# Feature-major norms in a long one-core kernel: sums of squares with tokens on partitions, root and reciprocal on four columns, factors spread by a product with a diagonal

## What is computed

```python
def rmsnorm(x, g):
    xf = x.astype(jnp.float32)
    y = xf * lax.rsqrt(jnp.mean(xf * xf, axis=-1, keepdims=True) + EPS)
    return (y * g.astype(jnp.float32)).astype(x.dtype)
```

## Time and profile before

| | |
|---|---|
| median of three runs | 2881.63 us (2880.54 to 2885.57) |
| the profiled execution's own time | 2886.34 us |
| its span | 2884.3 us |
| mean granted TensorE clock | 0.895 |
| TensorE busy / VectorE busy / ScalarE busy | 2425.5 / 1237.0 / 937.1 us |
| chain that ended last: TensorE / DMA / VectorE / ScalarE | 59% / 29% / 7% / 3% |

### The profile page before, as it was taken

One profiled execution on the slowest core, in us unless ns is written; L12 is line 12 of the kernel. 1 busy time (PEld: TensorE's weight loads), 2 busy tenths in 40 slices (PEclk: granted clock), 3 DMA queues, 4 the chain that ended last, 5 costly groups with the idle time before them and its releaser, 6 DMA issues.

```text
span 2884.3 us, 37990 instructions
## 1 busy us (share of the span) xinstructions
PE 2425.5 (84%) x16498; PEld 1682.2 (58%) x16498; DVE 1237.0 (43%) x1751; ACT 937.1 (32%) x1522; POOL 60.1 (2%) x36
## 2 busy tenths in 40 slices
PE   7999998666666676666688889999999998987998
PEld 7897785111111111111367778889788787976787
DVE  4567652000010000000365655567754656855654
ACT  4556541000000000000244444445444443733442
POOL 0000010000000000000000000000000000022000
PEclk9999998867767777676898999999999999999999
DMA  6553467999999999999624246565655654422452
GB/s 214 172 149 132 132 234 310 418 418 416 416 418 418 418 417 416 418 418 418 249 91 116 89 137 213 193 214 164 215 194 180 200 175 161 143 68 76 161 194 98
DMA packets 309927, 698.09 MB, mean 242 GB/s; under 512 B 35425, under 2 KB 211809, under 8 KB 275073
## 3 DMA queue, kind: packets, MB, share of 16 engines
q1 hardware_dynamic: 307456, 681.78, 63.7%
q0 software_dynamic: 2016, 13.67, 1.3%
q10 hardware_dynamic: 288, 0.22, 0.0%
HBM read 694.58 MB, written 1.05 MB: 241 GB/s over the span
## 4 chain that ended last, share of the span: by engine, by line
PE 59%; DMA 29%; DVE 7%; ACT 3%; issue 1%; SPq 1%; DVEq 0%; ACTq 0%
PE ps L560 16%; PE ps L561 15%; PE ps L562 15%; DMA af<-in_w_exp_gate 12%; DMA af<-in_w_exp_up 10%; DMA af<-in_w_exp_down 6%; PE ps L1567 2%; PE ps L2328 1%; PE ps L1598 1%; DVE ar L533 1%; PE ps L828 1%; PE ps L1110 1%; PE ps L1949 1%; SPq L491 1%; PE ps L960 1%
## 5 line engine op out<-in xcount | busy, mean ns | idle before, releaser
L560 PE MATMUL ps<-ar 128*128 128x512 f32 (+1 forms) x2688 | 944.5, 351 | 45.5 <-ACT ar L850 17.5
L561 PE MATMUL ps<-ar 128*128 128x512 f32 (+1 forms) x2688 | 925.0, 344 | 0.0
L562 PE MATMUL ps<-ar 128*128 128x512 f32 (+1 forms) x2688 | 924.6, 344 | 0.0
L533 DVE TENSOR_TENSOR ar<-af,ar 128x1024 fp32r<-128x1024 f32 x520 | 610.6, 1224 | 317.3 <-ACT ar L522 317.0
L560 PEld LDWEIGHTS ps<-ar 128*128 128x128 f32 x2688 | 516.5, 192 | 123.9 <-DVE ar L873 13.8
L522 ACT ACTIVATE ar<-af 128x1024 fp32r<-128x1024 f32 x520 | 516.2, 1049 | 157.5 <-PE ps L562 154.6
L562 PEld LDWEIGHTS ps<-ar 128*128 128x128 f32 x2688 | 516.8, 192 | 59.1
L561 PEld LDWEIGHTS ps<-ar 128*128 128x128 f32 x2688 | 517.8, 193 | 55.7 <-issue 0.5
L1567 PE MATMUL ps<-af 128*32 128x512 f32 x2048 | 369.0, 818 | 183.9 <-DMA af<-in_w_exp_up 92.1
L1567 PEld LDWEIGHTS ps<-af 128*32 128x32 f32 x2048 | 50.9, 125 | 485.4 <-DMA af<-in_w_exp_up 237.0
L1598 PE MATMUL ps<-af 128*32 128x512 f32 x1024 | 176.1, 804 | 95.2 <-DMA af<-in_w_exp_down 81.1
(11 more groups left out here) (279 smaller groups left out, 1597.4 us busy)
## 6 DMA issues: line engine op xcount, KB each, us to landing
af<-in_w_exp_gate SPq DMA_DIRECT2D x128, 1024.0 KB, 25.4
af<-in_w_exp_up SPq DMA_DIRECT2D x128, 1024.0 KB, 24.8
af<-in_w_exp_down SPq DMA_DIRECT2D x128, 1024.0 KB, 21.4
af<-in_ffn_w_in SPq DMA_DIRECT2D x88, 1024.0 KB, 5.8
af<-in_ffn_w_out SPq DMA_DIRECT2D x44, 1024.0 KB, 5.1
af<-in_w_in SPq DMA_DIRECT2D x33, 1024.0 KB, 5.2
af<-in_sgu_w_in SPq DMA_DIRECT2D x16, 1024.0 KB, 7.1
af<-in_w_out SPq DMA_DIRECT2D x12, 1024.0 KB, 5.1
```

What stands on the lines that cost most here:

```text
L533: e.tensor_tensor(self.WL[load.pair][:, c], self.base(i)[:, c], f_(self.WH[load.pair][:, c]), ALU.subtract).then_inc(*self.dve.inc(("lo", ...
L560: e.matmul(o, lh, rh, start=start, stop=False, skip_group_check=True)
L561: e.matmul(o, lh, rl, start=False, stop=False, skip_group_check=True)
L562: return e.matmul(o, ll, rh, start=False, stop=stop, skip_group_check=True)
```

## The change

In t_rms the operands change places. The squares of 128 tokens are now the stationary operand and two columns of the matrix of 1/1024 are the moving one, so that 16 products of 2 columns (8 groups by 2 halves of the tokens) take the place of 8 products of 256 columns; the mean squares of the tokens land on partitions, in four columns of PSUM. The root (a_sd) and the reciprocal (v_rstd) are then taken of 128 x 4 values, in a small tile SD. To bring the factors back along the free axis on all partitions, VectorE builds two 128 by 128 diagonal matrices (identity times factor times 1024) in RSTD, and TensorE multiplies each by the matrix of 1/1024 (the new t_spread: two products of 128 columns) into a PSUM bank, which v_normed reads in place of RSTD. For mem the spread stands behind the first half of the projection dak; for the other six it stands right behind the sums. The bank for it is one more out of the ring, so dak's quarters are in other banks than before.

```diff
--- before.py
+++ after.py
@@ -252,7 +252,7 @@
-        self.RSTD, self.SM2 = sm[:, 512:768], sm[:, 768:1024]
+        self.RSTD, self.SM2, self.SD = sm[:, 512:768], sm[:, 768:1024], sm[:, 504:508]
         self.IDN = self.C("ident")
         self.where = {}
         self.plan()
@@ -820,15 +820,27 @@
 
 
     def t_rms(self, e, name, tmp, ring, fs=range(8), first=True, last=True):
+
         if first:
             self.rms_free = self.take(ring.next(), name, (self.act, (name, "sd")))
         for n, f in enumerate(fs):
-            for w in self.Tw.new(*self.rms_free, self.act.val((name, "sq", f // 2))):
-                e.wait_ge(*w)
-            m = e.matmul(self.bank(name)[:, 0:T], self.C("ones"), F(tmp)[:, f, :], start=first and n == 0, stop=last and n == len(fs) - 1,
-                         skip_group_check=True)
+            for tt in range(2):
+                for w in self.Tw.new(*self.rms_free, self.act.val((name, "sq", f // 2))):
+                    e.wait_ge(*w)
+                m = e.matmul(self.bank(name)[:, 2 * tt:2 * tt + 2], F(tmp)[:, f, tt * P:(tt + 1) * P], self.C("ones")[:, 0:2],
+                             start=first and n == 0 and tt == 0, stop=last and n == len(fs) - 1, skip_group_check=True)
         if last:
             m.then_inc(*self.pe.inc(("ps", name)))
+
+    def t_spread(self, e, name, ring):
+
+        b = ring.next()
+        free = self.take(b, (name, "r"), (self.dve, (name, "o", 7)))
+        for tt in range(2):
+            for w in self.Tw.new(*free, self.dve.val((name, "diag", tt))):
+                e.wait_ge(*w)
+            m = e.matmul(self.ps[:, b, tt * P:(tt + 1) * P], self.C("ones"), self.RSTD[:, tt * P:(tt + 1) * P], start=True, stop=True)
+        m.then_inc(*self.pe.inc(("ps", name, "r")))
 
     def a_square(self, e, name, src, tmp, j, ready):
         for w in self.Aw.new(*ready):
@@ -852,19 +864,24 @@
     def a_sd(self, e, name, eps):
         for w in self.Aw.new(self.pe.val(("ps", name)), self.dve.val("eps")):
             e.wait_ge(*w)
-        e.activation(self.RSTD, self.bank(name)[:, 0:T], ACT.Sqrt, bias=self.EPS[eps]).then_inc(*self.act.inc((name, "sd")))
+        e.activation(self.SD, self.bank(name)[:, 0:4], ACT.Sqrt, bias=self.EPS[eps]).then_inc(*self.act.inc((name, "sd")))
 
     def v_rstd(self, e, name):
         for w in self.Vw.new(self.act.val((name, "sd"))):
             e.wait_ge(*w)
-        e.reciprocal(self.RSTD, self.RSTD).then_inc(*self.dve.inc((name, "rstd")))
+        e.reciprocal(self.SD, self.SD).then_inc(*self.dve.inc((name, "rstd")))
+        for tt in range(2):
+            for w in self.Vw.new(self.dve.val((name, "rstd"))):
+                e.wait_ge(*w)
+            e.tensor_scalar(self.RSTD[:, tt * P:(tt + 1) * P], self.IDN, self.SD[:, 2 * tt:2 * tt + 1], 1024.0, ALU.mult,
+                            ALU.mult).then_inc(*self.dve.inc((name, "diag", tt)))
 
     def v_normed(self, e, name, src, dst, gain, pair=None, dst_ready=()):
         for f in range(10):
             if f < 8:
-                for w in self.Vw.new(self.dve.val((name, "rstd")), *dst_ready):
-                    e.wait_ge(*w)
-                e.scalar_tensor_tensor(out=F(dst)[:, f, :], in0=F(src)[:, f, :], scalar=self.V(*gain(f)), in1=self.RSTD,
+                for w in self.Vw.new(self.pe.val(("ps", name, "r")), *dst_ready):
+                    e.wait_ge(*w)
+                e.scalar_tensor_tensor(out=F(dst)[:, f, :], in0=F(src)[:, f, :], scalar=self.V(*gain(f)), in1=self.bank((name, "r"))[:, 0:T],
                                        op0=ALU.mult, op1=ALU.mult).then_inc(*self.dve.inc((name, "o", f)))
             if f >= 2 and pair:
                 g = f - 2
@@ -1150,6 +1167,7 @@
         for w in self.Tw.new(self.first_all):
             e.wait_ge(*w)
         self.t_rms(e, "n1", self.B(9), KB)
+        self.t_spread(e, "n1", KB)
         daq = self.t_proj(e, "daq", 4, H, self.halves("n1"), DB, self.by_act("daq"))
         for c in range(3):
             next(daq)
@@ -1157,7 +1175,10 @@
             e.wait_ge(*w)
         self.t_rms(e, "mem", self.B(9), Ring(2, 3))
         run(daq)
-        run(self.t_proj(e, "dak", 4, H, self.halves("n1"), KB, self.by_act("dak")))
+        dak = self.t_proj(e, "dak", 4, H, self.halves("n1"), KB, self.by_act("dak"))
+        next(dak)
+        self.t_spread(e, "mem", KB)
+        run(dak)
         run(self.t_rows(e, "dav", H, self.halves("n1"), KB, self.rows_by(act, "dav")))
         self.end(self.pe, "da_in")
 
@@ -1514,6 +1535,7 @@
         KB, EB, TB = Ring(*range(8)), Ring(0, 1, 2, 3), Ring(4, 5, 6, 7)
         pe, act, dve, ps = self.pe, self.act, self.dve, self.ps
         self.t_rms(e, "ffn", self.B(6), KB, (6, 7), first=False)
+        self.t_spread(e, "ffn", KB)
         b = KB.next()
         free = self.take(b, "logits", (dve, "logits"))
         for k in range(8):
@@ -1745,7 +1767,9 @@
         DB, KB, OB, RB = Ring(0, 1), Ring(*range(8)), Ring(6, 7), Ring(4, 5)
         dve, H = self.dve, self.H
         self.t_rms(e, "final1", self.B(9), KB, (0, 1, 4, 5, 2, 3, 6, 7))
+        self.t_spread(e, "final1", KB)
         self.t_rms(e, "norm20", self.B(9), KB)
+        self.t_spread(e, "norm20", KB)
 
         def rope(name, dst, j, free_of, ready):
             b = RB.next()
@@ -1790,6 +1814,7 @@
                             lambda: self.t_rms(e, after, self.B(9), KB, range(6), last=False)))
             self.end(self.pe, "layer" + n)
             self.t_rms(e, after, self.B(9), KB, (6, 7), first=False)
+            self.t_spread(e, after, KB)
         self.end(self.pe, "final2")
 
     def a_second(self, e):
```

## The result

| | before | after |
|---|---|---|
| median of six runs each | 2881.65 us (2880.54 to 2885.57) | 2895.59 us (2890.80 to 2902.83) |
| ratio | | 1.0047, 95% interval 1.0036 to 1.0058 |
| the profiled execution's own time | 2886.34 us | 2893.71 us |
| its span | 2884.3 us | 2891.3 us |
| mean granted TensorE clock | 0.895 | 0.890 |

The change makes the kernel slower by 13.9 us. VectorE has 7.5 us less to do and TensorE is busy for 23 us longer.

A forecast was written before the change was run, and what follows sets the result against it. Bound by the chain that ended last, with the norms' sums and reciprocals on it. Terms 0 (n1) + 2.5 (mem) + 2.05 (ffn, norm21, final2) + 1.6 (final1) + 1.1 (norm20) = +7.25, giving 2888.9 us; range 2879.5 to 2895.5.

The forecast's parts named there:

- Steps of a record: Narrow sums: each 2-column record steps at 0.112 us at clock 1.00 and 0.213 at 0.50, like the weight load.
- Root to first multiplication: Inside a norm, from root's start: 2.30 us becomes 2.0 cold or 1.65 warm, saving 0.3 or 0.65.
- The small items of the new chain: Shorter root to multiplication at ffn, norm21, final2, final1, norm20, against mem's spread (+0.45) and bank wait (+0.3).
- n1's sums: First norm: sums cold, some 1 to 2 us later, covered by 4.12 us of TensorE idle time; cost 0.
- The clock: TensorE's granted clock, the deciding term: narrow sums neither raise it nor, less surely, hold it; like idle time.
- the pair: final1 and norm20: sums partly or wholly cold, +1.9 and +1.4; with the shorter chain +1.6 and +1.1.
- the three splits: ffn, norm21, final2, 24 narrow records between projection halves: +0.1 and clock loss 1.0 each, three times 1.1, +3.3.
- The step that failed: Last sum: +7.25 us, reckoned against the profiled 2886.34 us, added to the median 2881.6, giving 2888.9 us.
- The projection behind norm20: Restart of the projection after norm20's sums: cold before and after, so no cost was added.
- Rival 3: Clock falls at each of the three splits and stays low over second halves: +14, 2895.6 us; chance 0.15.
- Rival 1: Clock goes by busy time alone and narrow sums hold it: -3.4, 2878.2 us, no measurable change; chance 0.15.
- Rival 2: Faster: shorter root and reciprocal reach the chain at all seven norms: -6.6, 2875.0 us; chance 0.05.

The follow-up runs named there:

- all-wide run: The changed kernel with all 112 sums moving 128 columns instead of 2: 2883.13 us, 0.9996 to before; repeated on another chip: 2884.51 us, 0.9996.
- the repeated one: The changed kernel run and profiled again with no edit: 2895.67 us, ratio 1.0040 to the kernel before.

## Why the prediction was right, and where it was not

The sign and its mechanism were right. The median lies at the upper edge of the range, 0.1 us above it, and 6.7 us above the forecast, so the sizes were not.

- **Steps of a record, right.** 19 records in 2.00 us at 1.00 and 32 in 6.70 at 0.50: 0.11 and 0.21, as taken from the earlier trace rows.
- **Root to first multiplication, nearly right.** 2.11 us cold where the sum had 2.0, so 0.2 saved and not 0.3; the wait behind the second diagonal was 1.12 where the sum had 0.8, and the root (0.26 for 0.295) and the diagonals (0.48 for 0.57) gave part of that back. At 1.00, in the all-wide run, the four records of the spread take 0.71 us for 1.22. The small items of the new chain came to -1.1 us in the prediction (gains of 1.85, and 0.75 for mem's spread and bank); the all-wide runs give -1.2 (0.9996, -4.0 to +1.4). n1's sums end later, and TensorE still waits for the memory's squares for 2.60 us, of 4.12: cost 0, as forecast.
- **The clock, right in kind, too small.** The rest of the forecast, the sums with the clock in and behind them, was 1.8 us for mem, 1.9 + 1.4 for the pair and 3.3 for the three splits, 8.4 in all. The sums themselves came near it: final1's took 5.07 us for 5.6, norm20's 7.00 for 6.8, mem's 6.32 for 6.8. Behind mem's the projection was at 0.50 for 4.5 us, which at 0.44 a microsecond is 2.0 where the sum had 1.2. Measured narrow against wide it is some 13 us by the runs, and by the profiles 3.0 for mem, 4.5 for the pair and 3.4 for norm21 and final2, which had 2.2. Each of the three was forecast lower than it came out, by about as much as the profiles are good to; that their sum was too small the runs show.
- **The step that failed** is the last line of the sum: "so the forecast of the median is 2881.6 + 7.25". The clock's price had been read off one profiled execution, in which norm20's sums ran at 0.50 in the middle (5.42 us; wide sums take 3.7 to 3.8 where the clock stays up) and mem's began at 0.50 for 5.8 us. Against that execution +7.25 was nearly exact: the profile of the change is 7.4 us longer. That closeness is partly luck, since 1.4 us of the 7.4 arose in the third block, where nothing is changed, and the six executions of the changed kernel spread over 12 us. But the execution was 4.7 us over its median, and those low stretches belong to what made it slow, as far as the table shows. A difference against such a profile should not be added to the median. Only one profile of before exists, so where in it the 4.7 us lay stays open in part.
- **The projection behind norm20, costed at nothing.** "The restart of the projection is cold before and after": it was, but the clock came back after 6.3 us and not after 5.0; 1.3 us at 0.44 is 0.6. In the all-wide run it started at 1.00 and had 3.4 us at 0.50.
- **Splits.** The forecast took 1.0 for each, with a fall that might or might not come. In the profile of after it came at final2, and at neither of the others; in the repeated one at norm21. Over the six profiles with narrow splits there are 7 falls in 18 places, none of them at ffn and in no profile at all three. Rival 3, a fall at every one, is excluded; its time, 2895.6, is that of the result by chance.
- **Rival 1 is refuted.** By it the change would have saved 3.4 us, and it cost 13.9; wide sums in the same places took the loss away. The narrow sums did not hold the clock where TensorE had no gap before or in them (last section), and did not raise it at norm20. Against drops in mid-kernel the Trainium skill, page "TensorE: Matmul & The Clock Gate", asks in "Why this matters for your kernels" that TensorE have no long idle gaps between its bursts. For products of 2 columns the rows at final2 do not agree, though the profile counts TensorE as busy throughout; for those of 128 columns between the halves (clock at 1.00 behind them) they do. Rival 2 falls with it.

## What to carry to other kernels

A swap of operands that makes the moving one narrow saves no time where the step of a record is the same for few columns as for 128 (0.11 us at 1.00 and 0.21 at 0.50 here), and can take TensorE's clock away for itself and for the wide work behind it; widening the same products to 128 columns cost nothing here and gave the loss back. Price the clock against several executions, or at least ask first whether the one profile lies on its median, and never add a difference from an untypical profile to a median. And before an awkward layout is built to shrink an expensive operation, look for an instruction that makes it unnecessary: here that was worth 12 us, and the new layout with wide sums 1 us, which the runs do not tell from nothing.

## What was unexpected of the hardware

A busy TensorE lost its clock without one gap. TensorE alone in the changed kernel, at final2: wide products of the first half, the 24 narrow records, and the wide products of the second half.

```profile
1707.50:1711.70 4.20, 4.20 (x38) 1.00 0.74 246
1711.80:1714.30 2.50, 2.50 (x24) 1.00 0.44 42
1714.40:1715.30 0.90, 0.90 (x9) 1.00 0.99 348
1715.50:1718.40 2.90, 2.90 (x16) 0.50 0.53 185
```

It is busy for all of these 10.5 us, and the clock falls only when the narrow products are over, in the midst of 256-column ones. So the price of narrow work stands at the work behind it, on another line. It does not fall every time. In the six profiles in which the sums between the halves are narrow, it fell in or behind them in 7 of 18 places, each time before TensorE's next idle gap. Where they have 128 or 256 columns, in the other six profiles, it fell in none of 18.
